# The state space stage takes the sample's tiles first, and gate and norm of mixing's first tile run inside it

## The reference, cut to what matters

```python
for each sequence:
    y_f = ssd_scan(xh, dt_f, A[0], Bg, Cg)                     # forward over chunks of 128 tokens
    y_b = rev(ssd_scan(rev(xh), rev(dt_b), A[1], rev(Bg), rev(Cg)))
    y = y_f + y_b + d_skip[:, None] * xh
    y = y.reshape(b, s, 512) * silu(z)                         # gate
    y = y * rsqrt(mean(y*y, axis=-1) + 1e-5) * ssm_norm_w      # norm
    x = layer_norm(ALPHA * x + concat([attn, y]) @ w_out)
```

## Time and profile before

| | |
|---|---|
| Median of three runs | 3353.73 us (3353.0 to 3358.99) |
| The profiled execution | 3345.05 us |
| Its span | 3343.2 us |
| PE busy, PE weight loads, DVE, ACT, POOL | 99%, 92%, 68%, 56%, 12% of the span |
| State space stage | about 586.7 to 697.9 us |
| Mixing | about 697.9 to 876.8 us |
| Experts | from there to the end |

### The profile page before, as it was taken

The page is one execution under the profiler, slowest core; times in us unless marked ns, Lnnn a source line. Parts: engine busy times, 40 slices in busy tenths (PEclk is TensorE's granted clock), DMA queues, the critical chain, the costliest instruction groups (busy, mean ns, idle before and its releaser), DMA issues.

```text
span 3343.2 us, 59167 instructions
## 1 busy us (share of the span) xinstructions
PE 3295.3 (99%) x20263; PEld 3069.1 (92%) x20263; DVE 2289.1 (68%) x3811; ACT 1876.3 (56%) x3211; POOL 391.7 (12%) x394
## 2 busy tenths in 40 slices
PE   9999999999799999999999999999999999999997
PEld 7889899889798999999898999999898999999896
DVE  6521277688876767767676767767676767677687
ACT  4222377632365656656565656656565656656576
POOL 0000175532000000000000000000000000000013
PEclk9999999999999999999999999999999999999999
DMA  5334345254578777777777777777777777777786
GB/s 189 141 134 157 110 114 169 77 213 164 187 237 245 233 241 238 240 238 240 232 246 245 232 246 238 240 238 239 235 243 239 237 249 235 243 236 230 238 292 237
DMA packets 251025, 721.67 MB, mean 216 GB/s; under 512 B 55648, under 2 KB 71056, under 8 KB 250400
## 3 DMA queue, kind: packets, MB, share of 16 engines
q1 hardware_dynamic: 233856, 661.92, 60.7%
q0 software_dynamic: 16560, 57.27, 5.9%
q10 hardware_dynamic: 432, 0.10, 0.0%
HBM read 657.09 MB, written 66.16 MB: 216 GB/s over the span
## 4 chain that ended last, share of the span: by engine, by line
PE 72%; DVE 1%; issue 0%; POOL 0%; DMA 0%; POOLq 0%; ACT 0%; DVEq 0%
PE moe_gu L2481 33%; PE moe_gu L2482 15%; PE moe_dnp L2499 5%; PE moe_dnp L2500 5%; PE moe_dns L2494 5%; PE moe_dns L2495 5%; PE moe_dns L2496 5%; PE moe_dns L2466 0%; PE moe_dns L2467 0%; DMA moe_xg_s<-tmp_h,moe_grow_s 0%; DVE rtr_found L2886 0%; DVE rtr_affT L2888 0%; DVE rtr_found L2884 0%; POOL moe_rstd L2451 0%; POOLq L2221 0%
## 5 line engine op out<-in xcount | busy, mean ns | idle before, releaser
L2481 PE MATMUL moe_gu<-moe_xgT,moe_whi 128*128 128x384 f32 x5632 | 1610.0, 360 | 0.3 <-DVE moe_xgT L2733 0.3
L2711 DVE TENSOR_TENSOR moe_wlo<-moe_raw,moe_whi 128x1024 fp32r<-128x1024 f32 x1056 | 1292.0, 1224 | 450.8 <-ACT moe_whi L2595 449.1
L2482 PE MATMUL moe_gu<-moe_xgT,moe_wlo 128*128 128x192 f32 x5632 | 1410.9, 251 | 0.0
L2595 ACT CAST moe_whi<-moe_raw 128x1024 fp32r<-128x1024 f32 x1056 | 1107.6, 1049 | 378.4 <-PE moe_dnp L2500 371.4
L2482 PEld LDWEIGHTS moe_gu<-moe_xgT,moe_wlo 128*128 128x128 f32 x5632 | 1077.1, 191 | 0.6
L2481 PEld LDWEIGHTS moe_gu<-moe_xgT,moe_whi 128*128 128x128 f32 x5632 | 1057.4, 188 | 1.1 <-issue 0.5
L2494 PE MATMUL moe_dns<-moe_whi,moe_hid 128*128 128x512 f32 x704 | 274.4, 390 | 0.0
L2495 PE MATMUL moe_dns<-moe_whi,moe_hid 128*128 128x512 f32 x704 | 274.0, 389 | 0.0
L2496 PE MATMUL moe_dns<-moe_wlo,moe_hid 128*128 128x512 f32 x704 | 274.0, 389 | 0.0
L2499 PE MATMUL moe_dnp<-moe_whi,moe_hid 128*128 128x512 f32 x704 | 274.0, 389 | 0.0
L2500 PE MATMUL moe_dnp<-moe_wlo,moe_hid 128*128 128x512 f32 x704 | 274.0, 389 | 0.0
(11 more groups left out here) (421 smaller groups left out, 4291.7 us busy)
## 6 DMA issues: line engine op xcount, KB each, us to landing
moe_raw<-in_w_ffn SPq DMA_DIRECT2D x1056, 512.0 KB, 4.1
res_early<-in_w_in SPq DMA_DIRECT2D x10, 1024.0 KB, 6.0
tmp_qkT<-res_raw POOLq DMA_DIRECT2D x24, 256.0 KB, 2.3
res_early<-tmp_qkT SPq DMA_DIRECT2D x16, 384.0 KB, 6.5
res_raw<-tmp_qkT SPq DMA_DIRECT2D x16, 384.0 KB, 6.5
res_early<-tmp_xbc SPq DMA_DIRECT2D x12, 512.0 KB, 3.8
res_early<-in_x SPq DMA_DIRECT2D x12, 512.0 KB, 4.9
tmp_h<-res_early SPq DMA_DIRECT2D x12, 512.0 KB, 2.7
```

Of the source, the lines that this page charges most:

```text
L2481: pe.matmul(out[:, a, 0:2 * CAP], whi[c][:, j, :], x, start=(n == 0), stop=False)
L2482: mm = pe.matmul(out[:, a, 0:CAP], wlo[c][:, j, :], x[:, 0:CAP], start=False, stop=(n == KD - 1))
L2595: act.copy(whi[c][:], raw[c][:]).then_inc(hi_done, 1)
L2711: dve.tensor_tensor(wlo[c][:], raw[c][:], whi[c][:].bitcast(F32), ALU.subtract).then_inc(lo_done, 1)
```

## The change

The state space stage takes the sample's eight tiles in steps 0 to 7 and the prompt's four in steps 8 to 11: `ssd_tile(t)` gives the tile of step t, and all addresses that depend on the tile use it. The steps that open a sequence are now 0 and 8 (`FIRST_STEP`), those that close one 7 and 11. With this, tile 11 is complete after step 7. `near()` and `far()` run one step earlier, at the end of steps 7 and 8. At the end of step 9 (`GATED`) DVE gates tile 11, ACT sums its squares behind the spreads of that step, and POOL makes the root behind its output addition; DVE applies the norm at the end of step 10. These instructions, and three unused multiplications, go from mixing's start, and SP raises the semaphores there that they would have raised. In the last step DVE adds the skip part to `yo` ahead of its wait for `psy`, and its addition of `psy` writes the tile of y itself, so that the addition behind the loop goes. One of the two unused multiplications at the stage's end goes.

```diff
 # stage_attend, SP
             for t in range(2):
-                sp.dma_start(xb[t], ... [:, :, P * t:P * t + P])
+                of = ssd_tile(t)
+                sp.dma_start(xb[t], ... [:, :, P * of:P * of + P])
+def ssd_tile(t):
+    return (t + FIRST_TILE[1]) % NT
 # stage_ssd
+    FIRST_STEP = (0, NT - FIRST_TILE[1])
-    SPARE_END = 2
+    SPARE_END = 1
-    LAST_NEAR = 8
+    LAST_NEAR = 7
+    GATED = FIRST_STEP[1] + 1
+        first = res["y"][:, NT - 1, :]
+        junk = a20.rearrange("p h e -> p (h e)")
 # ACT, body(t), behind spreads(t + 2)
+                if t == GATED:
+                    act.wait_ge(gated, 1)
+                    act.activation(junk, first, ACT.Square, accum_out=total[:]).then_inc(squared, 1)
 # POOL, at the start
+            pool.memset(half[:], -0.5).then_inc(half_set, 1)
+            pool.wait_ge(half_set, 1)
 # POOL, loop, behind out(t)
+                if t == GATED:
+                    pool.wait_ge(squared, 1)
+                    pool.tensor_scalar(root[:], total[:], 1.0 / SSM_W, RMS_EPS, ALU.mult, ALU.add).then_inc(rooted, 1)
+                    pool.wait_ge(rooted, 1)
+                    pool.tensor_tensor(root[:], root[:], half[:], ALU.pow).then_inc(rooted, 1)
 # DVE, body(t), ahead of the wait for y_mm
+                if t == NT - 1:
+                    dve.wait_ge(off_scaled, offs(t))
+                    dve.wait_ge(skip_ready, NT)
+                    dve.tensor_tensor(yo[s], yo[s], xskip[s], ALU.add).then_inc(skip_added, 1)
+                    dve.wait_ge(skip_added, 1)
                 dve.wait_ge(y_mm, t + 1)
 ...
-                    dve.tensor_tensor(yo[s], yo[s], psy[:], ALU.add).then_inc(yo_ready, 1)
+                    to = by_heads(res["y"][:, ssd_tile(t), :]) if t == NT - 1 else yo[s]
+                    dve.tensor_tensor(to, yo[s], psy[:], ALU.add).then_inc(yo_ready, 1)
 # DVE, end of body(t), behind near() and far()
+                if t == GATED:
+                    dve.wait_ge(y_out, FIRST_STEP[1])
+                    dve.tensor_tensor(first, first, z0, ALU.mult).then_inc(gated, 1)
+                if t == NT - 2:
+                    dve.wait_ge(rooted, 2)
+                    dve.scalar_tensor_tensor(first, first, root[:], res["normw"][:], ALU.mult, ALU.mult).then_inc(normed, 1)
 # DVE, behind the loop
-            dve.wait_ge(skip_ready, NT)
-            dve.wait_ge(yo_ready, NT)
-            dve.tensor_tensor(res["y"][:, NT - 1, :] ..., yo[1], xskip[1], ALU.add).then_inc(y_out, 1)
 # stage_mix
+            for of in (gated, squared, rs_tmp, rs_ready, mix_ssm):
+                sp.sem_inc(of, 1)
             load_c(1)
 ...
-            turn_over(pe, po[:, 0, :], table[:, 0:P], table[:, 0:512], SPARE_START)
             turn(0)
 ...
-            squares(0)
 ...
-            root_gate(0)
 ...
-            gate(0)
             dve.memset(wide[:], 0.0).then_inc(wide_ready, 1)
-            norm(0)
```

More of the change, by code:

```diff
@@ L976, in _ @@
             for t in range(2):
-                sp.dma_start(xb[t], dram["xbc"].rearrange("(c p) t -> p c t", p=P)[:, :, P * t:P * t + P]).then_inc(xb_in, 16)
+                of = ssd_tile(t)
+                sp.dma_start(xb[t], dram["xbc"].rearrange("(c p) t -> p c t", p=P)[:, :, P * of:P * of + P]).then_inc(xb_in, 16)
             sp.wait_ge(score_mm, ITEMS * (HEADS - 1))
@@ L1215, in stage_ssd @@
         ex2 = [res["early"][:, last + NT * HEADS * i:last + NT * HEADS * i + NT * HEADS].rearrange("p (t h) -> p t h", t=NT) for i in range(2)]
+        first = res["y"][:, NT - 1, :]
+        junk = a20.rearrange("p h e -> p (h e)")
+        total, root, half = (m.small(name, [P, 1]) for name in ("total", "root", "half"))
         psx = m.ps("psx", [P, 512])
@@ L1266, in stage_ssd @@
         mixed = m.sem("mixed")
+        skip_added = m.sem("skip_added")
+        gated = m.sem("gated")
+        squared = m.sem("squared")
+        half_set = m.sem("half_set")
+        rooted = m.sem("rooted")
+        normed = m.sem("normed")
         fold_mm = m.sem("fold_mm")
@@ L1272, in opens @@
         def opens(t):
-            return t in FIRST_TILE
+            return t in FIRST_STEP
         def closes(t):
-            return t + 1 in (FIRST_TILE[1], NT)
+            return t + 1 in (FIRST_STEP[1], NT)
         def offs(t):
@@ L1317, in _ @@
                     sp.wait_ge(off_mm, offs(t - 2))
-                sp.dma_start(xb[t % 2], src[:, :, P * t:P * t + P]).then_inc(xb_in[t % 2], 16)
+                sp.dma_start(xb[t % 2], src[:, :, P * ssd_tile(t):P * ssd_tile(t) + P]).then_inc(xb_in[t % 2], 16)
                 if t == 3:
@@ L1405, in _ @@
                 to, at = (pso, 0) if k == 0 else (psy, k - 1) if k < 5 else (psf, 0)
-                mm = pe.transpose(to[:].rearrange("p h e -> p (h e)")[:, P * at:P * at + P], runs[:, k, :], ident[:])
+                mm = pe.transpose(to[:].rearrange("p h e -> p (h e)")[:, P * at:P * at + P], runs[:, ssd_tile(2 * k) // 2, :], ident[:])
                 if k in (0, NT // 2 - 1):
@@ L1455, in body @@
                 act.wait_ge(sb_mm, t + 1)
-                act.copy(stb[:, t, :, :], pss[:]).then_inc(stb_ready, 1)
+                act.copy(stb[:, ssd_tile(t), :, :], pss[:]).then_inc(stb_ready, 1)
                 if t + 1 < NT:
@@ L1488, in weighted @@
                 for d in range(2):
-                    pool.tensor_tensor(xst[s][:, d], xtok[s][:], over(wdt[:, d, t, :]), ALU.mult).then_inc(xst_ready, 1)
+                    pool.tensor_tensor(xst[s][:, d], xtok[s][:], over(wdt[:, d, ssd_tile(t), :]), ALU.mult).then_inc(xst_ready, 1)
             def skipped(t):
@@ L1498, in out @@
                 pool.wait_ge(skip_ready, t + 1)
-                pool.tensor_tensor(res["y"][:, t, :].rearrange("p (h e) -> p h e", e=HD), yo[t % 2], xskip[t % 2], ALU.add).then_inc(y_out, 1)
+                pool.tensor_tensor(by_heads(res["y"][:, ssd_tile(t), :]), yo[t % 2], xskip[t % 2], ALU.add).then_inc(y_out, 1)
             def empty(s):
@@ L1545, in body @@
                     after(dve, y_out, t - 1)
-                    dve.tensor_tensor(yo[s], pso[:], over(ex[:, FROM_START, t, :]), ALU.mult).then_inc(off_scaled, 1)
+                    dve.tensor_tensor(yo[s], pso[:], over(ex[:, FROM_START, ssd_tile(t), :]), ALU.mult).then_inc(off_scaled, 1)
                     if not closes(t):
-                        dve.tensor_tensor(Sf, Sf, over(ex[:, ALL_F, t, :]), ALU.mult).then_inc(sf_scaled, 1)
+                        dve.tensor_tensor(Sf, Sf, over(ex[:, ALL_F, ssd_tile(t), :]), ALU.mult).then_inc(sf_scaled, 1)
                 weights(t, 1)
@@ L1556, in body @@
                     else:
-                        dve.wait_ge(sf_scaled, carries(t) - sum(i <= t for i in FIRST_TILE))
+                        dve.wait_ge(sf_scaled, carries(t) - sum(i <= t for i in FIRST_STEP))
                         dve.tensor_tensor(Sf, Sf, psf[:], ALU.add).then_inc(sf_ready, 1)
@@ L1633, in _ @@
                 body(t)
-            dve.wait_ge(skip_ready, NT)
-            dve.wait_ge(yo_ready, NT)
-            dve.tensor_tensor(res["y"][:, NT - 1, :].rearrange("p (h e) -> p h e", e=HD), yo[1], xskip[1], ALU.add).then_inc(y_out, 1)
             dve.wait_ge(fold_lo, 1)
             dve.wait_ge(stb_ready, NT)
-            dve.wait_ge(y_out, NT)
+            dve.wait_ge(y_out, NT - 1)
+            dve.wait_ge(yo_ready, NT)
+            dve.wait_ge(normed, 1)
 def by_heads(of):
@@ L1709, in stage_mix @@
         stb, sx, att, y = res["stb"], res["ex"], res["att"], res["y"]
-        SPARE_START, SPARE_ROWS = 3, 2
+        SPARE_ROWS = 2
         table = sx[:].rearrange("p n t h -> p (n t h)")
```

## The result

The changed kernel took 3357.94 us (median of 20 runs, 3351.27 to 3363.99), the kernel before in the same session 3352.05 (20 runs, 3346.64 to 3359.51): a ratio of 1.0017, interval 1.0010 to 1.0023. The forecast was 1.9 us faster, with a range of 3346 to 3357; the time lies above the range, on the other side of no change. (The sum had started from a median of three runs, 1.7 us above that of the 20.)

What follows compares the result with a forecast made beforehand. The prediction took the experts' matrix multiplications to bound the kernel, so savings had to start them earlier. Its terms, -0.79 (stage's end), -1.4 (mixing's start) and +0.25 (state space loop), gave -1.9 us: median 3351.8, range 3346 to 3357.

Steps and rivals of the forecast that it cites:

- The likeliest case: Whole kernel: the sum as it stands, -1.9 us, median 3351.8, own range 3349.4 to 3354.5; chance 0.45.
- more falls: Rival, state space stage and border: additional clock falls cost 1.6 to 1.9 each; +1.6 us, 3355.3; chance 0.15.
- The places named for more falls: The six folding steps, which get other neighbours, and the border to mixing, which loses four of five spares.
- At a border a fall costs little: Border to mixing: a clock fall there costs little, because the wait for wlo covers most of it.
- End of the stage, -0.79: State space stage's end: skip addition hidden, one spare less, mixing starts 0.79 us earlier; 0 to 0.97.
- Far merge, -0.9: State space loop: merge one step earlier, the addition then starts within 0.1 us of POOL's weighting; gain 0.9 us.
- The alternative sum: State space stage by the shared-port rule: addition costs 0, not 0.4, norm 0.75, not 0.3; sum same within 0.05.
- Gate and square, +0.85: State space steps 9 and 10: ACT's square delays the exponentials; cost 0.6, or 1.05 with the gate's wait; 0.85 taken.
- Norm, +0.3: End of step 10: DVE's norm stands ahead of the last tile's scaling; cost 0 to 0.75 us, 0.3 taken.
- Order, 0: State space loop: sample first keeps the number of all additions, loads and copies; no term in the sum.
- Start of mixing, -1.4: Mixing's start: first projection at S+3.2 instead of S+4.68, second half at S+11.6; gain 1.4 us, 0.6 to 2.65.
- as long as the data are there: Mixing: PE is dense from the first projection, so time won ahead of it is kept if the data are there.

Runs made afterwards that it cites:

- after: Profiled execution of the changed whole kernel: 3358.99 us, against 3345.05 us for the profiled execution of the kernel before.
- e2: Changed kernel, experts left out, forward state (psf) formed between psy's multiplications and folding in the folding steps: 902.22 us.
- f2: Changed kernel, experts left out, next tile's products run between psy's multiplications and the folding: 905.19 us.
- c2: Changed kernel with the experts' stage left out, a copy of mixing's result to the output in its place: 903.69 us.
- c1: Kernel before with the experts' stage left out, a copy of mixing's result to the output in its place; the yardstick: 898.18 us.
- c3: Kernel before, experts left out, with only the order of the tiles changed (sample first): 904.18 us.
- e3: Kernel before, experts left out, with the merge of the attention's last tile moved into folding steps 4 and 5: 898.33 us.
- c4: Changed kernel, experts left out, with gate, square, root and norm of tile 11 and three spares back at mixing's start: 901.41 us.
- g_near4: Whole kernel before with the merge in steps 4 and 5, last addition ahead of its wait, one spare at the stage's end: 3349.63 us, ratio 0.9998.
- d: Kernel before and changed kernel, experts left out, keeping 8 of 64 folding multiplications: 892.41 and 894.90 us.
- h: Kernel before with sample-first order, experts left out, folding moved to steps 4 to 9 or 3 to 8: 903.92 and 911.50 us.
- d3: Kernel before, experts left out, backward state (pss) formed between psy's multiplications and folding, ACT's order adapted: 906.80 us.
- d4: Changed kernel, experts left out, backward state (pss) formed between psy's multiplications and folding, ACT's order adapted: 906.02 us.
- e1: Kernel before, experts left out, forward state (psf) formed between psy's multiplications and folding in the folding steps: 902.02 us.
- f: Kernel before and changed kernel, experts left out, next tile's products run between psy's multiplications and folding: 900.42 and 905.19 us.

## Why the prediction was wrong

The step that failed first is the term without a price in the sum: the clock. The likeliest case kept the falls as they were; "more falls" stood among the rivals with 0.15, two falls and 3355.3. Low time rose by 11.4 us a run (48.3 - 36.9), more than three falls, worth 4.3 to 5.7 us. The second is the gain: of the 1.9 us that the sum had, nothing came, mainly because far merge and start of mixing gained nothing. The places named for more falls were right: the folding steps, and the border. In three of the six profiles of the changed form (after, e2, f2) a fall begins within 3 us of mixing's start, in none of the fourteen others. "At a border a fall costs little" was right, for another reason: it hid under the wait for the C tile (0.61 in after, 1.51 in c2, which had no fall there), not under that for wlo. It made the last spare 0.6 longer, but held mixing's start back by 0.15 only (1.65 behind the last multiplication into psy, 1.50 in c2).

The rest, point by point, at full clock:

- *End of the stage, -0.79*: -0.55. Right in kind.
- *Far merge, -0.9*: 0. This step failed in the start that it gave an addition. I counted two DVE operations fewer ahead of it and had it start beside POOL's weighting, within 0.1 us. It started 0.44 behind, DVE having worked without a pause, and took the full 1.53, as in the earlier trace rows:
```profile
681.82 0.69 DVE L1573 TENSOR_TENSOR res_v<-ssd_pso,res_ex 128x512 f32<-128x512 f32 x1
...
682.59 2.87 POOL L1509 TENSOR_TENSOR res_raw<-ssd_xtok,res_wdt 128x512 f32<-128x512 f32 x2 [2.08 <-ACT ssd_xtok L1449]
...
683.03 1.53 DVE L1562 TENSOR_TENSOR ssd_E<-ssd_E 128x512 f32<-128x512 f32 x1
...
685.33 1.80 PE L1414 MATMUL ssd_psy<-ssd_xtok,ssd_W 128*128 128x64 f32 x8 [1.42 <-DVE ssd_W L1566]
```
  The order of the two starts set the price, as the Trainium skill's rule (SBUF — State Buffer, section SBUF: two separate sides) has it: who starts first has the shared ports for the whole instruction, and the other is blocked. The trace agrees: this addition, 0.69 by itself, took 1.53 behind POOL's start, and in the kernel before one that started 0.44 ahead of it took 0.68:
```profile
678.34 0.68 DVE L1535 TENSOR_TENSOR ssd_E<-ssd_E 128x512 f32<-128x512 f32 x1
...
678.78 2.14 POOL L1489 TENSOR_TENSOR res_raw<-ssd_xtok,res_wdt 128x512 f32<-128x512 f32 x2 [2.12 <-ACT ssd_xtok L1432]
```
  The alternative sum, which used that rule with the same wrong start, was as wrong.
- *Gate and square, +0.85*: +0.58. The square ran between spreads and exponentials, as forecast (first two rows below, from after).
- *Norm, +0.3*: +0.59, near the upper end. It took 1.04 beside POOL (third row), and PE's last wait for W grew from 0.59 to 1.26.
```profile
691.41 0.63 ACT L1481 ACTIVATE res_early<-res_att 128x512 f32<-128x512 f32 x1
...
692.04 1.07 ACT L1460 ACTIVATE ssd_E<-ssd_seg 128x512 f32<-128x512 f32 x2
...
697.92 1.04 DVE L1614 SCALAR_TENSOR_TENSOR res_att<-res_att,ssd_root,res_normw 128x512 f32<-128x512 f32 x1
```
- *Order, 0*: +0.2. The folding steps 3 and 4 take 9.13 each instead of 8.83 and 9.07; steps 7 and 8, where the closing and the opening now stand, are hardly shorter (7.17, 7.29), because a light step is not PE's. The order has a second price, which the sum did not see: steps 3 and 4 lose the spare time of PE, and a fall there costs 1.9 instead of 0.8 to 1.0.
- *Start of mixing, -1.4*: -0.25 in the profile of after, +0.3 in c2, both to PE's last multiplication of mixing; DVE's last operation of mixing came 0.6 and 0.05 earlier, counted from S. The first projection came as worked out, the second half in after (S+11.84) but not in c2 (S+12.36); the claim that the gain is kept "as long as the data are there" failed at the next C tile, which I had not followed. PE's earlier start ran into transfers that start from the same S.

Sum at full clock: 0.2 + 0.1 (far) + 0.58 + 0.59 - 0.55 = +0.9 in the stage and about 0 in mixing, where -1.9 was forecast. With the 4.3 to 5.7 of the clock that makes 5.2 to 6.6, beside 5.9 measured (3.4 to 7.7 by the interval of the ratio).

What stays open is why the clock falls more, and how much of it the order alone brings. c1 and c3, which differ in the order alone, have low times of 37.7 and 43.3 in five runs each, which overlap. Pooled, the prompt-first kernels c1 and e3 have 37.3 (standard error 1.2, ten runs), the sample-first c2 to c4 44.7 (1.9, fifteen); but e3 ran on another chip, c2 and c4 hold other edits, and the prompt-first g_near4, left out of this, had 40.8 (2.7, twelve). In the folding steps the clock was low for 3.4 to 10.2 us in the prompt-first profiles and for 10.2 to 20.5 in the sample-first ones. Falls of double length in folding steps appear in three of the four sample-first profiles in the loop's own order (after, c2, c3) and in none of the four prompt-first ones (before, c1, e3, g_near4). The amount of folding (d) does not explain it alone; the neighbours (h) could not be tested cleanly; keeping psy and folding apart (d3, d4, e1, e2) takes it away, but at longer steps, and f did not separate the two. The Trainium skill (TensorE: Matmul & The Clock Gate, section What's actually happening) says that the clock's decisions keep their own time, which does not start with the kernel. The runs agree: one and the same kernel (c3) had from 32 to 54 us at the low clock.

## What to carry to other kernels

A tuned loop can have its clock on the edge: before reordering it, look for stretches at the low level and for what PE ran just ahead of each, and price a few more of them as part of the sum and not as a rival. A fall, too, costs by its step: 0.8 to 1.0 us where PE had time to spare, up to 1.9 where it had none. Work on a second engine is free only in the steps that another engine sets: the same merge cost 1.5 us in a light step and nothing in a folding one, so look for the step and not for the engine's mean idle time. An earlier start is worth what the first transfer that starts with it allows: follow it until two tiles in a row stand where they stood.

## Hardware that I had not expected

- Experts with the same instructions take 151.3 or 152.9 to 153.1 us at a granted clock of 1.00; which of the sixteen do so, and how many (1, 5, 6 and 6), differs between the four profiles of whole kernels. What sets the pace is not known from these runs.
- The kernel before had medians of 3342.4, 3342.5 and 3342.6 us on three chips and 3349.8 and 3351.0 on two others, at low times of 35 to 39 us. Each chip had one session, so chip and session are not told apart: kernels are compared within one session.
- The state space stage ran at the full clock throughout in d3 and still took 10 us more than that of c1 with its falls taken off (116.6 against 106.6): fewer falls are not by themselves a gain.
